# Expert matrices loaded with consecutive rows in one partition, in a two-block transformer kernel with a mixture of 64 experts

## The chip, the core and the metric

The kernel runs on one core of a Trainium2 chip, alone. The metric is device time in microseconds (us) of one execution. The core has a matrix engine (PE, with its own weight loads PEld), a vector engine (DVE), a scalar engine (ACT), GpSimd (POOL), a queue engine that issues most DMAs (SP), and 16 DMA engines that the queues share. SBUF has 128 partitions; a matmul contracts over partitions and writes one of eight PSUM banks.

## What is computed

A sequence of 256 tokens of width 1024 passes two blocks, all in float32. The first block and the mixer of the second are not touched. What matters is the last stage, a mixture of 64 experts with top-2 routing (`t` are the normalised tokens, `gate` the two routing weights):

```
hid = silu(t[tokens of e] @ w_gate[e]) * (t[tokens of e] @ w_up[e])      # 1024 -> 512
out[tokens of e] += gate * (hid @ w_down[e])                              # 512 -> 1024
```

`w_gate` and `w_up` are (64, 1024, 512), `w_down` is (64, 512, 1024): each matrix is 2 MB, 192 of them. A row of `w_gate` or `w_up` is 2 KB in DRAM, a row of `w_down` 4 KB, and a matrix is one contiguous block. A last normalisation follows.

## The kernel before

The first 40% of the time is dense work: 47 panels of weights go through `raw`, are split in two parts on ACT and DVE, and PE multiplies them (lines L763 and L1200). The change does not touch that.

The expert stage takes experts in **pairs**, 32 rounds. Every expert has 64 slots (`SLOTS`), so that a pair fills 128 rows; if an expert had more tokens a further pass would run, guarded by `fullest > SLOTS`. In this input none runs: each line of the loop shows 32 rounds. One round on PE, in `experts` from L1078 on, is, in program order:

- gate and up products (L1090): for each of two matrices, 8 chunks `k` of the width, 2 experts, 64 columns of `xeT` stationary and 512 columns of the matrix moving; the two experts use different halves of the PE columns. Before each matrix PE waits for its DMA (`pair_landed`).
- two transposes of `pick_g` (L1096), then, when DVE has multiplied the silu by the up product (`h_e`, L1652), **four transposes of `h_e`** (L1101): slice `c` is columns `128 c` to `128 c + 127` of the 512. ACT copies the result into `heT` (L708).
- `gather` for the next pair (L1072): 16 matmuls that pick the pair's tokens out of **`t_rows`** with a 0/1 matrix; chunk `k` of `xeT` is columns `128 k` to `128 k + 127` of `t_rows`.
- down products (L1112), four chunks `c` of `heT`, and, when both halves of `y_e` are copied out (L1659 on DVE, L712 on ACT), the scatter into the four accumulating banks (L1120).

`nc.tensor.transpose(out, in_, identity)` loads `in_` as the stationary operand (PEld LDWEIGHTS) and moves the identity.

Since chunk `k` of the stationary operand and chunk `k` of the matrix meet in one matmul, partition `p` of both must hold the same row of the matrix. Before, that row is `128 k + p`.

**Loads.** `load` on SP (L356 to L374) issues two DMAs, one for each expert of a pair, into `slots` (gate, up and down) or, for the gate matrices of odd rounds, into `areas`. Gate is so double-buffered and issued a round ahead of up and down, which have one buffer each. The order on SP is up, down, gate of the round after, each behind a wait that its buffer is free: up behind the last up product (L1090), down and gate behind the last down product (L1112). For all but the first two rounds the DMA has a condition: an expert without tokens is not loaded.

**`t_rows`** is made once (L1565): DVE multiplies the normalised rows `xn` by the gain, two instructions of 128x1024, after its part of the transposes for the router (L1188) and while PE runs the router's product (L1049). `t_ready` lets DVE go on to `choose`, and is one of two things for which the load of the second gate pair waits (the other is the router's product). Then come DVE's routing steps (L1570 to L1622), the first `choose` (L1634), the first gather, and the first round.

Of the kernel before, what the change touches and what calls it, by code (L numbers as in the profile page):

```python
# [22 lines left out]
ALU = mybir.AluOpType  # L23
# [3 lines left out]
P = 128  # L27
# [3 lines left out]
KT = D // P  # L31
# [57 lines left out]
def program(nc, x_in, p_in, norm_mix_g, w_in, w_sgu, b_sgu, ln_v_g, ln_v_b, rel_bias, w_out, norm_ffn_g,  # L89
# [24 lines left out]
    with ExitStack() as ctx:  # L114
# [29 lines left out]
        ident = sb("ident", [P, P])  # L144
# [28 lines left out]
        xn = rows_area(9)  # L173
# [28 lines left out]
        t_rows = rows_area(0)  # L202
        zeros = area(4)[:, 0:256].bitcast(mybir.dt.bfloat16)
        gains = rows_area(5)
        routerw = area(4)[:, 512:512 + KT * (EG + NE)].rearrange("p (k n) -> p k n", k=KT)
        xeT = area(1)[:, 0:1024].rearrange("p (k s) -> p k s", k=KT)
        h_e = area(1)[:, 1024:1536]
# [9 lines left out]
        banks = [ctx.enter_context(nc.psum_tensor(f"bank{b}", [P, 512], F32)) for b in range(8)]  # L217
# [87 lines left out]
        def expert_panel(w, e, odd):  # L305
            s = {"gate": 0, "up": 2, "down": 4}[w] + e
            place = area(6 + 2 * e, 2) if w == "gate" and odd else slots[:, s, :]
            return place.rearrange("p (k n) -> p k n", k=4 if w == "down" else 8)
# [12 lines left out]
        def _(sp):  # L321
# [15 lines left out]
            for q in range(2 * NP):  # L337
                p, (kind, j) = q // 2, PANELS[q // 2]
                k = shape(p)[0] // 2
# [19 lines left out]
            def load(w, i, pair, odd, beyond):  # L359
                weights, used = {"gate": (w_gate, gated), "up": (w_up, upped), "down": (w_down, downed)}[w]  # L360


                tokens = [None if beyond is None else tokens_of(pair, e) for e in range(2)]
                if isinstance(i, int) and i == 0:
                    sp.wait_ge(panel_done, NP)
                elif isinstance(i, int) and w == "gate":
                    sp.wait_ge(t_ready, 1)
                    sp.wait_ge(routed, 1)
                else:
                    sp.wait_ge(used, i - 1 if w == "gate" else i)  # L370
                for e in range(2):
                    cond = {} if beyond is None else {"cond": tokens[e] > beyond}
                    sp.dma_start(expert_panel(w, e, odd), weights[0, 2 * pair + e].rearrange("(k p) n -> p k n", p=P),
                                 **cond).then_inc(pair_landed["odd_gate" if w == "gate" and odd else w, e], 16)  # L374

            def tokens_of(pair, e):
# [353 lines left out]
        def _(pe):  # L730
            mm, turn_tile = nc.tensor.matmul, nc.tensor.transpose
# [108 lines left out]
            for g in range(GROUPS):  # L840
                last = turn_tile(banks[6 + g // 4][:, P * (g % 4):P * (g % 4) + P], w_s[:, g, :], ident[:, :])
# [8 lines left out]
            for m in range(MT):  # L850
                for half in range(2):
                    for g in range(4 * half, 4 * half + 4):
                        last = mm(banks[4 + 2 * m + half][:, P * (g % 4):P * (g % 4) + P], w_sT[:, g, :],
                                  v_rows[:, m, P * g:P * g + P], start=True, stop=True)
# [25 lines left out]
            for k in range(2):  # L880
                for m in range(MT):
                    last = turn_tile(banks[0][:, S * k + P * m:S * k + P * m + P], p_rows[:, m, P * k:P * k + P], ident[:, :])
            last.then_inc(p_turned, 1)
            for j in range(8):
                p = AT["ff2", j]
                pe.wait_ge(hid_ready, 4 * (j // 2) + 4)
                for k in range(KT):
                    if k % 4 == 0:
                        pe.wait_ge(w_ready, 2 * p + k // 4 + 1)
                    for m in range(MT):  # L890
                        last = product(banks[4 + 2 * m + j % 2][:, :], (hid_hi, hid_lo),
                                       (every, KT * (j // 2) + k, slice(P * m, P * m + P)), parts(p), (every, k, every),
                                       j < 2 and k == 0, j >= 6 and k == KT - 1)
# [3 lines left out]
            p = AT["pp", 0]  # L897
            pe.wait_ge(w_ready, 2 * p + 2)
            pe.wait_ge(pT_ready, 1)
            for half in range(2):  # L900
                for m in range(MT):
                    for k in range(2):
                        last = product(banks[4 + 2 * m + half][:, :], (pT_hi, pT_lo), (every, k, slice(P * m, P * m + P)),
                                       parts(p), (every, k, slice(512 * half, 512 * half + 512)), k == 0, k == 1)
# [9 lines left out]
            for k in range(KT):  # L914
                last = product(banks[4][0:HEADS, 0:S], (dtw_hi, dtw_lo), (every, k, every), h, (every, k, every),
                               k == 0, k == KT - 1)
# [3 lines left out]
            for m in range(MT):  # L920
                last = turn_tile(banks[4][:, S + HEADS * m:S + HEADS * m + HEADS], dt_cols[:, P * m:P * m + P],
                                 ident[0:HEADS, 0:HEADS])
# [3 lines left out]
            p = AT["kv2", 0]  # L926
            w, b0 = parts(p), pair_of(p)
# [6 lines left out]
            for m in range(MT):  # L934
                for k in range(KT):
                    last = product(banks[b0 + 1][:, P * m:P * m + P], h, (every, k, slice(P * m, P * m + P)),
                                   w, (every, k, slice(2 * P, 3 * P)), k == 0, k == KT - 1)
# [33 lines left out]
            for m in range(MT):  # L971
                for half in range(2):
                    for c in range(4):
                        last = turn_tile(banks[2 * m + half][:, P * c:P * c + P], xc[:, 4 * half + c, P * m:P * m + P],
                                         ident[:, :])
# [10 lines left out]
            for g in range(SSD_G):  # L986
                last = turn_tile(banks[0][:, P + P * g:P + P * g + P], xc[:, 8 + g, 0:P], ident[:, :])
            last.then_inc(sums_made, 1)

            for m in range(MT):  # L990
                for g in range(SSD_G):
                    last = mm(banks[1][:, 256 * m + P * g:256 * m + P * g + P], xc[:, 8 + g, P * m:P * m + P],
                              xc[:, 10 + g, P * m:P * m + P], start=True, stop=True)
# [20 lines left out]
            for m in range(MT):  # L1014
                for q in range(4):
                    n = 4 * m + q
                    if n >= 2:
                        pe.wait_ge(seg_ready, n - 1)
                    for i in range(4):
                        last = mm(banks[n % 2][:, P * i:P * i + P], a[:, m, 4 * q + i:4 * q + i + 1].to_broadcast([P, P]),  # L1020
                                  upper[:, :], start=True, stop=True)
# [7 lines left out]
            for g in range(SSD_G):  # L1029
                last = mm(banks[g][:, :], b_tok[:, g, :], xde[:, 512 * g:512 * g + 512], start=True, stop=True)  # L1030
# [3 lines left out]
            for g in range(SSD_G):  # L1034
                last = mm(banks[2 + g][:, :], xc[:, 10 + g, P:S], state[:, 512 * g:512 * g + 512], start=True, stop=True)
# [11 lines left out]
            for m in range(MT):  # L1047
                for k in range(KT):
                    last = mm(banks[0][:, 72 * m:72 * m + 72], hT[:, k, P * m:P * m + P], routerw[:, k, :],  # L1049
                              start=(k == 0), stop=(k == KT - 1))  # L1050
# [25 lines left out]
            def experts(half_i, odd, last_one=False):  # L1076

                i = 2 * half_i + odd  # L1078
                pe.wait_ge(xe_a, i + 1)
                pe.wait_ge(xe_d, i + 1)  # L1080

                for w, bank, done in (("gate", banks[2], gated), ("up", banks[3], upped)):
                    for e in range(2):
                        if w == "gate":
                            pe.wait_ge(pair_landed["odd_gate" if odd else w, e], 16 * (half_i + 1))
                        else:
                            pe.wait_ge(pair_landed[w, e], 16 * (i + 1))
                    for k in range(KT):
                        for e in range(2):
                            last = mm(bank[SLOTS * e:SLOTS * e + SLOTS, :], xeT[:, k, SLOTS * e:SLOTS * e + SLOTS],  # L1090
                                      expert_panel(w, e, odd)[:, k, :], start=(k == 0), stop=(k == KT - 1))
                    last.then_inc(done, 1)

                pe.wait_ge(picked_g, i + 1)
                for m in range(MT):
                    last = turn_tile(banks[1][:, P * m:P * m + P], pick_g[:, m, :, :].rearrange("p e s -> p (e s)"),  # L1096
                                     ident[:, :])
                last.then_inc(put_turned, 1)
                pe.wait_ge(he_ready, i + 1)
                for c in range(4):  # L1100
                    last = turn_tile(banks[0][:, P * c:P * c + P], h_e[:, P * c:P * c + P], ident[:, :])  # L1101
                last.then_inc(he_turned, 1)
                pe.wait_ge(heT_ready, i + 1)
                pe.wait_ge(put_ready, i + 1)
                if not last_one:
                    gather(i + 1)
                for e in range(2):
                    pe.wait_ge(pair_landed["down", e], 16 * (i + 1))
                for c in range(4):
                    for half in range(2):  # L1110
                        for e in range(2):
                            last = mm(banks[2 + half][SLOTS * e:SLOTS * e + SLOTS, :], heT[:, c, SLOTS * e:SLOTS * e + SLOTS],  # L1112
                                      expert_panel("down", e, odd)[:, c, 512 * half:512 * half + 512],
                                      start=(c == 0), stop=(c == 3))
                last.then_inc(downed, 1)
                pe.wait_ge(ye_a, i + 1)
                pe.wait_ge(ye_d, i + 1)
                for m in range(MT):
                    for half in range(2):
                        last = mm(banks[4 + 2 * m + half][:, :], put[:, m, :], y_e[:, 512 * half:512 * half + 512],  # L1120
                                  start=False, stop=False)
                last.then_inc(scattered, 1)
# [20 lines left out]
        def _(dve):  # L1143
# [418 lines left out]
            dve.wait_ge(xn_a, 5)  # L1562
            dve.wait_ge(gains_loaded, 32)
            for m in range(MT):
                last = tt(t_rows[:, m, :], xn[:, m, :], gains[:, 0, :], ALU.mult)  # L1565
            last.then_inc(t_ready, 1)

            dve.wait_ge(consts_made, 1)
# [155 lines left out]
```

## Time and profile before

| | |
|---|---|
| three runs, median (lowest to highest) | 1771.02 us (1770.88 to 1771.63) |
| the profiled execution, first to last instruction | 1770.0 us |
| what lies around that span, by the median | 1.0 us |
| PE busy, share of the span | 1610.4 us, 91% |
| DVE, ACT busy | 552.4 us, 455.6 us |
| expert stage, first product to last scatter | 752 to 1759 us |
| moved by DMA over the span | 489.17 MB |

The page gives no total of its own for the profiled execution besides its span; its own time is the span and what lies around it, and that is why the two stand side by side. In the rows further down, a time with x32 or x1024 is the time of a group; "idle before" names what ended the wait. A MATMUL of float32 operands appears as two records, a transpose as one. In the chain of waits each row starts where its predecessor released it.

### The profile page before, as it was taken

What the parts mean: (1) busy time and instruction counts of PE and PEld (TensorE: products, weight loads), DVE (VectorE), ACT (ScalarE), POOL (GpSimd) and SP (SyncE); (2) the same over time, 40 slices, a digit from 0 to 9 for tenths busy, and PEclk for the clock granted to TensorE, in tenths of its full rate; (3) what the DMA queues carried; (4) which work ended last, traced back from release to release, by engine and by line L of the source; (5) the groups of instructions that cost most, each with busy time, mean ns of one, the idle gap of its engine ahead of it and who ended that gap; (6) DMA issues with size and microseconds to landing.
All of it is one profiled execution on the core that took longest, in us unless ns stands there. A gap on an engine that the chain in (4) does not pass through costs nothing.

```text
span 1770.0 us, 21051 instructions
## 1 busy us (share of the span) xinstructions
PE 1610.4 (91%) x8473; PEld 987.1 (56%) x8475; DVE 552.4 (31%) x936; ACT 455.6 (26%) x652; POOL 13.5 (1%) x30
## 2 busy tenths in 40 slices
PE   7999889999799979699999999999999999999996
PEld 5897779987689767534343343433434334343342
DVE  5755565544647976401011010110101101001012
ACT  5435545432535553101111011110111101111011
POOL 1000000000000000000000000000000000000000
PEclk9999989999899979799999999999999999999999
DMA  7554235554332213789899999999999999998994
GB/s 277 186 198 141 96 119 185 191 191 166 131 131 96 96 53 97 290 323 337 321 392 393 397 392 396 394 392 397 392 395 395 392 397 329 379 368 287 395 392 156
DMA packets 213002, 489.17 MB, mean 276 GB/s; under 512 B 6424, under 2 KB 8596, under 8 KB 212949
## 3 DMA queue, kind: packets, MB, share of 16 engines
q1 hardware_dynamic: 211764, 484.17, 74.6%
q0 software_dynamic: 1184, 4.26, 0.8%
q8 instruction: 37, 0.61, 0.2%
q14 instruction: 17, 0.13, 0.0%
HBM read 506.20 MB, written 1.08 MB: 287 GB/s over the span
## 4 chain that ended last, share of the span: by engine, by line
PE 74%; DVE 9%; ACT 3%; issue 2%; DVEq 0%; ACTq 0%
PE bank L1090 25%; PE bank L763 18%; PE bank L1112 13%; PE bank L1072 7%; PE bank L1120 7%; DVE areas L1659 1%; DVE areas L1652 1%; PE bank L1101 1%; ACT areas L708 1%; DVE w_lo L1200 1%; DVE h_lo L1190 1%; PE bank L746 1%; DVE areas L1450 1%; PE bank L1020 1%; PE bank L1010 0%
## 5 line engine op out<-in xcount | busy, mean ns | idle before, releaser
L1090 PE MATMUL bank<-slots,areas 128*64 128x512 f32 x1536 | 335.8, 593 | 1.1 <-DVE areas L1644 1.1
L1090 PEld LDWEIGHTS bank<-slots,areas 128*64 128x64 f32 x1536 | 109.8, 137 | 221.9 <-issue 221.9
L1200 DVE TENSOR_TENSOR w_lo<-raw,w_hi 128x2048 fp32r<-128x2048 f32 (+2 forms) x98 | 209.0, 2167 | 75.9 <-ACT w_hi L508 75.7
L1112 PE MATMUL bank<-slots,areas 128*64 128x512 f32 x1024 | 226.8, 595 | 0.7 <-ACT areas L708 0.7
L1652 DVE TENSOR_TENSOR areas<-bank,areas 128x512 f32<-128x512 f32 x32 | 22.1, 692 | 556.5 <-PE bank L1090 556.5
L508 ACT ACTIVATE w_hi<-raw 128x2048 fp32r<-128x2048 f32 (+2 forms) x98 | 173.6, 1816 | 62.3 <-PE bank L763 56.5
L763 PE MATMUL bank<-h_hi,w_hi 128*128 128x256 f32 x560 | 160.9, 287 | 0.2 <-DVE h_lo L1190 0.2
L763 PE MATMUL bank<-h_lo,w_hi 128*128 128x256 f32 x560 | 159.1, 284 | 0.0
L763 PE MATMUL bank<-h_hi,w_lo 128*128 128x256 f32 x560 | 159.1, 284 | 0.0
L1072 PE MATMUL bank<-areas 128*128 128x128 f32 x1024 | 125.5, 282 | 26.3 <-ACT areas L708 23.7
L763 PE MATMUL bank<-w_hi,h_hi 128*128 128x512 f32 (+1 forms) x344 | 138.4, 402 | 7.9 <-DVE h_lo L1190 3.0
L1112 PEld LDWEIGHTS bank<-slots,areas 128*64 128x64 f32 x1024 | 70.7, 137 | 132.6 <-issue 127.9
L1120 PE MATMUL bank<-areas 128*128 128x512 f32 x256 | 117.5, 602 | 28.3 <-DVE areas L1659 28.3
L1072 PEld LDWEIGHTS bank<-areas 128*128 128x128 f32 x1024 | 119.5, 196 | 33.7 <-issue 30.0
L763 PE MATMUL bank<-w_hi,h_lo 128*128 128x512 f32 (+1 forms) x344 | 134.1, 390 | 0.0
L763 PE MATMUL bank<-w_lo,h_hi 128*128 128x512 f32 (+1 forms) x344 | 134.0, 390 | 0.0
L1090 PE MATMUL bank<-areas 128*64 128x512 f32 x512 | 113.4, 595 | 0.0
L763 PEld LDWEIGHTS bank<-h_hi,w_hi 128*128 128x128 f32 x560 | 108.2, 193 | 2.1 <-issue 0.6
L763 PEld LDWEIGHTS bank<-h_lo,w_hi 128*128 128x128 f32 x560 | 108.3, 193 | 0.0
L763 PEld LDWEIGHTS bank<-h_hi,w_lo 128*128 128x128 f32 x560 | 108.1, 193 | 0.0
L1120 PEld LDWEIGHTS bank<-areas 128*128 128x128 f32 x256 | 46.0, 189 | 101.5 <-ACT areas L712 55.6
L706 ACT ACTIVATE areas<-bank 128x512 f32<-128x512 f32 x32 | 19.1, 598 | 310.4 <-PE bank L1090 310.4
(293 smaller groups left out, 1452.0 us busy)
## 6 DMA issues: line engine op xcount, KB each, us to landing
slots<-in_w_up_dram SPq DMA_DIRECT2D x64, 2048.0 KB, 16.9
slots<-in_w_down_dram SPq DMA_DIRECT2D x64, 2048.0 KB, 14.2
slots<-in_w_gate_dram SPq DMA_DIRECT2D x32, 2048.0 KB, 19.2
areas<-in_w_gate_dram SPq DMA_DIRECT2D x32, 2048.0 KB, 22.0
raw<-in_w_in_dram SPq DMA_DIRECT2D x42, 1024.0 KB, 6.0
raw<-in_w_ff_dram SPq DMA_DIRECT2D x32, 1024.0 KB, 5.3
raw<-in_w_out_dram SPq DMA_DIRECT2D x12, 1024.0 KB, 5.2
raw<-in_w_ple_gate_dram SPq DMA_DIRECT2D x4, 1024.0 KB, 5.5
```

The source lines that it names most:

```text
L508: last = act_(hi, source, ACT.Copy)
L706: act_(h_e, banks[2][:, :], ACT.Silu).then_inc(silu_ready, 1)
L708: act_(heT.rearrange("p c s -> p (c s)"), banks[0][:, :], ACT.Copy).then_inc(heT_ready, 1)
L746: last = turn_tile(banks[b][:, at:at + P], src[:, m, P * k:P * k + P], ident[:, :])
L763: last = mm(psum, a[i][a_at], b[j][b_at], start=(start and n == 0), stop=(stop and n == 2))
L1020: last = mm(banks[n % 2][:, P * i:P * i + P], a[:, m, 4 * q + i:4 * q + i + 1].to_broadcast([P, P]), upper[:, :], start=True, stop=True)
L1072: last = mm(banks[b][:, P * k:P * k + P], t_rows[:, m, P * (4 * b + k):P * (4 * b + k) + P], pick[:, m, :, :].rearrange("p e s -> p (e s)" ...
L1090: last = mm(bank[SLOTS * e:SLOTS * e + SLOTS, :], xeT[:, k, SLOTS * e:SLOTS * e + SLOTS], expert_panel(w, e, odd)[:, k, :], start=(k == 0) ...
L1112: last = mm(banks[2 + half][SLOTS * e:SLOTS * e + SLOTS, :], heT[:, c, SLOTS * e:SLOTS * e + SLOTS], expert_panel("down", e, odd)[:, c, 51 ...
L1120: last = mm(banks[4 + 2 * m + half][:, :], put[:, m, :], y_e[:, 512 * half:512 * half + 512], start=False, stop=False)
L1200: last = tt(lo, source, hi, ALU.subtract)
L1652: tt(h_e, banks[3][:, :], h_e, ALU.mult).then_inc(he_ready, 1)
```

## The change

Three edits. Partition `p` of an expert matrix now holds rows `8 p` to `8 p + 7` (gate, up) or `4 p` to `4 p + 3` (down) instead of every 128th row. That is one run of 16 KB in DRAM and in SBUF instead of eight of 2 KB or four of 4 KB. To match, chunk `c` of `heT` holds the elements `4 p + c` of `h_e`, read by the transposes with a step of four float32 (16 bytes); and `t_rows` is stored permuted, so that its chunk `k` holds the elements `8 p + k`. The permutation is made by the multiplication at L1565, which reads both operands with a step of eight float32 (32 bytes) and writes in order. No instruction, wait or buffer is added or taken away.

```diff
@@ -370,7 +370,7 @@
                 for e in range(2):
                     cond = {} if beyond is None else {"cond": tokens[e] > beyond}
-                    sp.dma_start(expert_panel(w, e, odd), weights[0, 2 * pair + e].rearrange("(k p) n -> p k n", p=P),
+                    sp.dma_start(expert_panel(w, e, odd), weights[0, 2 * pair + e].rearrange("(p k) n -> p k n", p=P),
                                  **cond).then_inc(pair_landed["odd_gate" if w == "gate" and odd else w, e], 16)
@@ -1098,7 +1098,7 @@
                 for c in range(4):
-                    last = turn_tile(banks[0][:, P * c:P * c + P], h_e[:, P * c:P * c + P], ident[:, :])
+                    last = turn_tile(banks[0][:, P * c:P * c + P], h_e.rearrange("s (p c) -> s c p", c=4)[:, c, :], ident[:, :])
                 last.then_inc(he_turned, 1)
@@ -1562,7 +1562,8 @@
             for m in range(MT):
-                last = tt(t_rows[:, m, :], xn[:, m, :], gains[:, 0, :], ALU.mult)
+                last = tt(t_rows[:, m, :].rearrange("t (k p) -> t k p", k=KT), xn[:, m, :].rearrange("t (p k) -> t k p", k=KT),
+                          gains[:, 0, :].rearrange("t (p k) -> t k p", k=KT), ALU.mult)
             last.then_inc(t_ready, 1)
```

## Rows read from the trace of the kernel before

**Rows 1.** Waits of PE over the whole span: total us, times, longest us

```profile
PE bank L1120 <- DVE areas L1659: 28.3, 32, 0.9
PE bank L1072 <- ACT areas L708: 23.7, 31, 0.8
PE bank L1101 <- DVE areas L1652: 15.8, 32, 0.5
PE bank L831 <- DMA areas<-in_norm_ffn_dram: 10.6, 1, 10.6
```

**Rows 2.** Chain of waits, one round and the next start: start us, us, what

```profile
1225.72 13.91 PE bank L1090 x64
...
1239.72 0.70 DVE areas L1652
...
1240.47 0.67 PE bank L1101 x4
...
1241.16 0.61 ACT areas L708
...
1241.89 3.83 PE bank L1072 x32
1245.72 7.04 PE bank L1112 x32
...
1252.79 0.70 DVE areas L1659
...
1253.63 3.67 PE bank L1120 x8
1257.30 13.91 PE bank L1090 x64
```

**Rows 3.** DMA from 1029 to 1061 us: rate in 40 slices, packets, queue

```profile
GB/s 384 387 389 384 394 381 389 384 417 410 410 410 410 410 410 410 410 410 410 410 397 389 387 384 394 381 389 384 389 384 387 389 381 394 382 392 384 389 384 389
DMA packets 5230, 12.61 MB, mean 394 GB/s; under 512 B 96, under 2 KB 96, under 8 KB 5230
...
q1 hardware_dynamic: 5230, 12.61, 104.3%
```

**Rows 4.** Engines, clock and DMA by stretch, 911.6 to 1445 us

```profile
911.60:1445.00 533.40, 496.89 (x2405) 210.04 (x2402) 52.21 (x102) 62.42 (x85) 0.00 (x0) 1.00 1.04 394
```

**Rows 5.** SP's up and gate issues, start us, us; landings by window

```profile
892.58 1.82 SPq L373 DMA_DIRECT2D slots<-in_w_up_dram  x2
slots<-in_w_up_dram SPq DMA_DIRECT2D x2, 2048.0 KB, 15.6
...
1414.83 11.31 SPq L373 DMA_DIRECT2D slots<-in_w_gate_dram  x2
...
1432.24 5.04 SPq L373 DMA_DIRECT2D slots<-in_w_up_dram  x1
slots<-in_w_up_dram SPq DMA_DIRECT2D x1, 2048.0 KB, 19.3
...
1447.05 0.91 SPq L373 DMA_DIRECT2D areas<-in_w_gate_dram  x2
```

**Rows 6.** Chain of waits, the round whose up matrices those are

```profile
1446.77 13.91 PE bank L1090 x64
```

**Rows 7.** Timeline, DVE and PE around the making of `t_rows`

```profile
726.86 2.35 DVE L1565 TENSOR_TENSOR areas<-areas 128x1024 f32<-128x1024 f32 x2
...
727.63 3.76 PE L1049 MATMUL bank<-areas,hT 128*128 128x72 f32 x32 [0.98 <-DVE hT L1188]
...
731.50 0.31 DVE L1570 COPY areas<-bank 128x144 f32<-128x144 f32 x1 [2.29 <-PE bank L1049]
...
737.68 12.54 SPq L373 DMA_DIRECT2D areas<-in_w_gate_dram  x2
```

**Rows 8.** DVE by shape: two reduces of 128 elements, in order and strided

```profile
L1255 DVE TENSOR_REDUCE peak<-soft 128x1 f32<-128x128 f32 x32 | 8.8, 276 | 0.0
...
L1592 DVE TENSOR_REDUCE areas<-areas 128x16 f32<-128x128 f32 x1 | 0.4, 380 | 0.0
```

**Rows 9.** Weight loads by shape in one round, 1190 to 1230 us: busy us, mean ns

```profile
L1072 PEld LDWEIGHTS bank<-areas 128*128 128x128 f32 x32 | 3.6, 192 | 1.0 <-issue 1.0
...
L1101 PEld LDWEIGHTS bank<-ident,areas 128*128 128x128 f32 x4 | 0.4, 141 | 0.7 <-DVE areas L1652 0.7
```

**Rows 10.** Source line L1101: duration ns min/median/max of its matmuls

```profile
L1101 PE MATMUL bank<-ident,areas x128: 272/273/331, 766.8 to 1746.0; 128*128 128x128 f32 x128
```

**Rows 11.** The page's DMA queues: packets, MB, share of 16 engines

```profile
q1 hardware_dynamic: 211764, 484.17, 74.6%
```

## The prediction

> **What bounds the kernel now.** I read the waits of PE first, because PE is busy for 91% of the span. In the expert stage its three largest waits are for engines that have just been handed its own result, 0.5 to 0.9 us each, 32 times [rows 1]. The only DMA in the list is a small vector at the start of the kernel (L831). PE does not wait for an expert matrix once.
>
> The chain of waits says the same for one round [rows 2]: from 1225.72 to 1257.30 us, 31.58 us, it is products on PE for 29.1 us (13.91 + 0.67 + 3.83 + 7.04 + 3.67), three copies or multiplications of 0.6 to 0.7 us on DVE and ACT, and small gaps. No DMA stands in it, and 32 such rounds are some 57% of the span.
>
> Next I asked how close the DMA is behind. In one saturated round the queues move at 381 to 397 GB/s (mostly 387) while gate and up pass, whose runs are 2 KB, and at 410 while down passes, with runs of 4 KB [rows 3]. The mean is 394 GB/s, also over seventeen rounds at once, with the engines' share at 104% (packets overlap a little) [rows 3, 4]. A round needs six matrices of 2.097 MB, 12.58 MB; at 394 that is 31.94 us. PE asks for them every 31.58 us. **The DMA is 1% too slow, and this cannot be seen in PE's waits because it is bought from a reserve.** The last up transfer of this stretch is issued at 1432.24 and lands 19.3 us later [rows 5], at 1451.5; its product begins in the middle of the block that starts at 1446.77 [rows 6], at 1446.77 + 6.96 = 1453.7. So 2.2 us of reserve are left. Seventeen rounds earlier the pair issued from 892.58 on lands 15.6 us after issue [rows 5], the second about 1 us behind the first, so at some 909; its product begins at 1453.7 - 17 x 31.58 = 916.8: a reserve of 8 us. It falls by 5.8 / 17 = 0.34 us a round, which is 31.94 - 31.58 again. Then, at 1447, two gate issues take 0.91 us instead of 11.31 [rows 5]: I read this as a load left out for an expert without tokens, after which the queue catches up. The reserve runs low, and never out.
>
> **The DMAs.** 192 transfers change their runs from 2 or 4 KB to 16 KB. Per engine a run of 2 KB takes 2048 x 16 / 387 = 84.7 ns, one of 4 KB takes 4096 x 16 / 410 = 159.8 ns. The second 2 KB cost 75.1 ns, which leaves 9.6 ns for each run. My estimate from these two: 16 KB take 9.6 + 8 x 75.1 = 610 ns, 430 GB/s, and a round's matrices take 29.3 us instead of 31.9. The lower bound of the gain is nothing: the queue may cut the runs as before. In the span either is worth **0 us**, because no product waits now. What covers the transfers is PE's 31.58 us; if the cover were gone they would cost the 0.34 us by which a round's 31.94 exceed it. SP issues as many DMAs in the same order behind the same waits. It would be held less long by a full queue (1 to 12 us per pair now), which nobody waits for.
>
> **`t_rows`.** The two DVE instructions end at 726.86 + 2.35 = 729.21. The next DVE instruction starts at 731.50, when PE's router product lets it [rows 7]. So 2.29 us are free. The step of 32 bytes has one relative in the trace: the reduce at L1592 reads 128 elements with that step and takes 380 ns, one of 128 elements in order (L1255) takes 276 [rows 8]. That is 104 / 128 = 0.81 ns per element (some of it may be its 16 outputs instead of one). For 2 x 1024 elements it makes 1.66 us if the two strided operands are read side by side: hidden. If they add up it is 3.32 us, of which 1.03 come onto the path, once. I take 0; bounds 0 and 1.0. The load behind `t_ready` waits for the same router product and is issued at 737.68 because the queue is full, so it does not move.
>
> **The transposes of `h_e`.** The four are on the chain, 0.67 us in each round [rows 2]. What changes is their weight load, now with a step of 16 bytes; the identity moves as before. A load takes 141 ns by its record, and those of the gather, of the same 128 columns but for a float32 product, 192 [rows 9]. The first of the four matmuls takes 0.33 us by its record (the maximum) [rows 10], so the others follow at (0.67 - 0.33) / 3 = 0.11 us, and the gather's at (3.83 - 0.33) / 31 = 0.11 as well [rows 2]: the longer load of the gather costs no pace. So a load 51 ns longer costs next to nothing per matmul, since it runs ahead under the one before; only the first of four, which waits for DVE, shows it. If a strided load takes as long as the gather's: 51 ns and 3 ns allowed for each of the other three make 0.06 us a round, 32 rounds, **2.0 us**. Lower bound: 0, no penalty. Upper bound: DVE's 1.81 ns per strided element, as if the memory set it. That is 1.00 in order, (1175 - 276) / (1024 - 128) from half of the 2.35 us and the 276 ns [rows 7, 8], plus 0.81. Then a load takes 128 x 1.81 = 232 ns, 122 more than the pitch of 110 for three of them; the first shows 232 less 53 (128 columns at one clock of 2.4 GHz, the granted clock being 1.00 [rows 4]), 179. That is 0.55 us a round, 18 us. I take 2.0, because the gather's loads are the nearest row: the same engine, the same port, at a lower pace per column.
>
> Row first, then the rule: no row of PE has a step, so the trace is silent on it. The Trainium skill (SBUF — State Buffer, under Door 1: The DMA port swizzle) says that SBUF has lines of 16 bytes, that two hits on a line are needed to hide the access, and that a new line for each access pays a penalty. By that rule all the `h_e` loads and the `t_rows` reads pay; the size is not given. The same paragraph also calls a stride of four float32 free, and by that only `t_rows` pays. DVE's 380 against 276 ns agrees with a penalty at 32 bytes.
>
> **Sum.** 0 + 0 + 2.0 = 2.0 us on the profiled execution: span 1770.0 to 1772.0, and with the 1.0 us around it 1773.0. The median shown, 1771.02, is that execution's span plus the same 1.0, so it serves as the base.
>
> **Rivals.**
> - *The strided loads leave their cover (slower).* Place: L1101, each round. Point: when a load takes more than about 0.11 us of the PE's port, because then three of four matmuls wait too. At DVE's extra 0.81 ns on top of one clock, 0.42 ns, a column, a load takes 157 ns: 104 + 3 x 47 = 0.25 us a round, 8 us, **1779 us**. At the upper bound **1789**. For: DVE shows a penalty, and PE would read faster than DVE. Against: loads run ahead, and a moderate penalty is covered. (It is what the Trainium skill's rule of lines, named above, would do here if its penalty is large.)
> - *The long runs are slower (slower).* Neighbouring partitions are then read 16 KB apart instead of 2 or 4, and their streams may meet in DRAM. The reserve of 8 us lasts 17 rounds as long as a round's matrices take under 31.58 + 8 / 17 = 32.05 us; it decides below 12.58 / 32.05, 392 GB/s. At 385 they take 32.7 us: 17 x 1.1 - 8, **+11 us**, 1782. Against: down, with longer runs, is the faster one now.
> - *The change does not reach the engines.* Runs are cut into 2 KB packets again and strides cost nothing: **1771.0**. Inside the forecast.
> - *Faster.* A shorter DMA stretch pays only if a product waits. Even if all of the 2.2 us reserve had been a hidden wait, it would be **1769**. Nothing in the waits speaks for it.
>
> **How the numbers follow.** A measurement of this kernel can tell about 0.2%, 3.5 us, from no change. Forecast (0 to 3.5 us slower, the third rival in it): 0.67. Loads out of their cover: 0.22. Long runs slower: 0.06. Faster by over 3.5 us: 0.05, for what I have overlooked. Slower is 0.22 + 0.06 = 0.28. The range 1770 to 1783 holds the forecast and the rivals up to half of their ends; some 0.16 lie outside. The forecast's own range is 1770 to 1774.5.
>
> **What would show it.** Right: packets on the queue fall from 211764 [rows 11] to under 100000, the DMA share in a round falls below 1.0, SP's issues get short, the block of 13.91 us stays as it is, L1101's matmuls take 0.67 to 0.75 us, L1565 takes 2.4 to 4.6 and DVE's wait before L1570 shrinks by as much. Wrong: L1101 over 0.8 us a round; a DMA among PE's waits; rounds under 31.5 us; or a matmul of L1090 that is quicker beside less traffic.

## The result, and the profile after

The changed kernel takes 1774.18 us (median of 20 runs, 1772.44 to 1776.99); the kernel before took 1771.22 in its 20 (1769.23 to 1774.10). The ratio is **1.0019, 95% interval 1.0012 to 1.0025**: 3 us slower. That is within the 0.2% that the prediction counts as no change, but twenty runs of each tell it from none. The forecast was 1773.0.

The chain of waits of the changed kernel, one round and the next start (start us, us, what), shows where it is:

```profile
1224.93 13.91 PE bank L1090 x64
...
1238.93 0.70 DVE areas L1653
...
1239.68 0.76 PE bank L1101 x4
...
1240.46 0.61 ACT areas L708
...
1241.19 3.83 PE bank L1072 x32
1245.03 7.04 PE bank L1112 x32
...
1252.09 0.70 DVE areas L1660
...
1252.93 3.67 PE bank L1120 x8
1256.60 13.91 PE bank L1090 x64
```

A round takes 31.67 us instead of 31.58, and one row differs from [rows 2]: L1101, 0.76 for 0.67. 32 x 0.09 = 2.9 us, which is the difference of the medians. (The spans of the two profiled executions, 1770.0 and 1770.8, differ by less because the dense stage of the second happened to end 2.2 us earlier: L1570 started at 731.50 before [rows 7], the same copy at 729.34 after.)

Weight loads and matmuls of L1101 by source line (duration ns min/median/max) answer to [rows 9, 10]:

```profile
L1101 PEld LDWEIGHTS bank<-ident,areas x128: 196/211/220, 764.6 to 1746.7; 128*128 128x128 f32 x128
L1101 PE MATMUL bank<-ident,areas x128: 283/284/387, 764.6 to 1746.8; 128*128 128x128 f32 x128
```

A load takes 70 ns more. The first matmul shows most of it (387 against 331), the others 11 ns each. DVE around `t_rows`, by timeline, answers to [rows 7]:

```profile
724.74 3.95 DVE L1565 TENSOR_TENSOR areas<-areas 128x1024 f32<-128x1024 f32 x2
729.34 0.31 DVE L1571 COPY areas<-bank 128x144 f32<-128x144 f32 x1 [0.65 <-PE bank L1049]
```

The two instructions take 1.60 us more together, and all of it comes out of the wait behind them, 2.29 us before and 0.65 now.

The DMA did what the change says. The page's queue row, and the stretches 1033.5 to 1048 us (no pause in it) and 911.6 to 1445 us (last three numbers: granted clock, DMA share, GB/s), to set beside [rows 11, 3, 4]:

```profile
q1 hardware_dynamic: 79028, 484.17, 68.8%
...
1033.50:1048.00 14.50, 14.50 (x66) 4.84 (x66) 0.00 (x0) 0.60 (x1) 0.00 (x0) 1.00 1.01 432
...
911.60:1445.00 533.40, 496.86 (x2397) 211.85 (x2394) 52.21 (x102) 62.42 (x85) 0.00 (x0) 1.00 0.95 397
```

The page has 211764 - 79028 = 132736 packets less. An expert's three matrices were 2560 runs and are now 384, 2176 less, and 132736 is 61 x 2176: each run of 16 KB is one packet, and 61 of the 64 experts are loaded, which bears out the prediction's reading that some loads are left out. A pair of gate issues on SP takes 1.01 us (at 1191.80), where the kernel before was held 9.83 (at 1192.75).

432 GB/s while it runs (I had 430), so a round's 12.58 MB need 29.1 us and the engines now pause, 95% instead of 104%. The mean stays at 397 because PE asks for no more. PE's busy time in the long stretch is 496.86 us for 496.89 before. The Trainium skill (DMA: Bandwidth & Descriptors, Specifications) gives 435 GB/s as the ceiling of the SBUF side: the 432 agree. It also gives some 358 GB/s as the limit of the memory side per core; with one core at work both kernels are over that.

### The profile page after: what moved, and what is told of

It reads as the page before. It is cut to its first block, busy times and chain, and to the rows that moved or that the text cites. A ratio compares the mean times of both kernels' runs of the same rounds, so it can differ in the third digit from the quotient of the medians.

```text
span 1770.8 us, 21053 instructions
## 1 busy us (share of the span) xinstructions
PE 1610.3 (91%) x8475; PEld 988.9 (56%) x8475; DVE 554.2 (31%) x936; ACT 455.5 (26%) x652; POOL 13.5 (1%) x30
## 3 DMA queue, kind: packets, MB, share of 16 engines
q1 hardware_dynamic: 79028, 484.17, 68.8%
## 4 chain that ended last, share of the span: by engine, by line
PE 74%; DVE 9%; ACT 3%; issue 2%; DVEq 0%; ACTq 0%
PE bank L1090 25%; PE bank L763 18%; PE bank L1112 13%; PE bank L1072 7%; PE bank L1120 7%; PE bank L1101 1%; DVE areas L1653 1%; DVE areas L1660 1%; ACT areas L708 1%; DVE w_lo L1200 1%; DVE h_lo L1190 1%; PE bank L746 1%; DVE areas L1450 1%; PE bank L1020 1%; PE bank L1010 0%
## 5 line engine op out<-in xcount | busy, mean ns | idle before, releaser
L1072 PE MATMUL bank<-areas 128*128 128x128 f32 x1024 | 125.5, 282 | 26.3 <-ACT areas L708 23.7
L1072 PEld LDWEIGHTS bank<-areas 128*128 128x128 f32 x1024 | 119.5, 195 | 32.2 <-issue 28.6
```

Source lines behind the costliest of these rows:

```text
L1072: last = mm(banks[b][:, P * k:P * k + P], t_rows[:, m, P * (4 * b + k):P * (4 * b + k) + P], pick[:, m, :, :].rearrange("p e s -> p (e s)" ...
```

## The experiments

**Which part costs, and does the rest do anything?** `loads_only` takes the new loads and puts the two reads back in order; `reads_only` is the other half. In both the operands don't match row for row, so the expert part of the output is another; the work is the same.

```diff
 loads_only, against the changed kernel
-                    last = turn_tile(banks[0][:, P * c:P * c + P], h_e.rearrange("s (p c) -> s c p", c=4)[:, c, :], ident[:, :])
+                    last = turn_tile(banks[0][:, P * c:P * c + P], h_e[:, P * c:P * c + P], ident[:, :])
...
+                last = tt(t_rows[:, m, :], xn[:, m, :], gains[:, 0, :], ALU.mult)
 reads_only, against the changed kernel
-                    sp.dma_start(expert_panel(w, e, odd), weights[0, 2 * pair + e].rearrange("(p k) n -> p k n", p=P),
+                    sp.dma_start(expert_panel(w, e, odd), weights[0, 2 * pair + e].rearrange("(k p) n -> p k n", p=P),
```

> All matrices are loaded in runs of 16 KB, but the transposes of h_e and the making of t_rows read in order as before, so the operands no longer match row for row: the result is another, the work is the same. Theory Reads (the strided weight loads at L1101 are the whole difference, 0.09 us in each of 32 rounds, and the DMA is worth nothing because no product waits for it): rounds of 31.58 us, L1101 0.67 us, time as before, 1771 within noise. Rival Loads (the long runs themselves slow the stage, for instance by writing 16 KB at a time into a partition that PE reads): rounds of 31.67 us with L1101 at 0.67, time some 3 us over before. Both: DMA at about 432 GB/s while busy, share in a round about 0.95.

> The loads are those of the kernel before (runs of 2 and 4 KB), the transposes and t_rows read with their steps: operands don't match row for row, the work is the same. Theory Reads: rounds of 31.67 us, L1101 0.76 us, weight loads 211 ns, time 3 us (0.17%) over before. The DMA still runs at 394 GB/s, but loses only 31.94 - 31.67 = 0.27 us of reserve a round instead of 0.34. Rival Loads: rounds of 31.58, time as before.

Measured: `loads_only` 1771.36 us, ratio 1.0003 (0.9994 to 1.0012); `reads_only` 1774.42, ratio 1.0015 (1.0006 to 1.0024), each against 1771.46 for the kernel before beside them. The intervals overlap slightly; the chains decide. `loads_only`, one round:

```profile
1224.25 13.91 PE bank L1090 x64
...
1239.00 0.67 PE bank L1101 x4
...
1255.84 13.91 PE bank L1090 x64
```

and `reads_only`:

```profile
1226.95 13.91 PE bank L1090 x64
...
1241.70 0.77 PE bank L1101 x4
...
1258.62 13.91 PE bank L1090 x64
```

Rounds of 31.59 and 31.67. The long runs neither help nor disturb; the reads are the difference.

**Which of the two reads?** `down_old` leaves `w_down` in its old layout, so that `h_e` is transposed in order, and keeps the permuted `t_rows`. Its result is unchanged.

```diff
 down_old, against the changed kernel
+                    sp.dma_start(expert_panel(w, e, odd), weights[0, 2 * pair + e].rearrange("(k p) n -> p k n" if w == "down" else "(p k) n -> p k n", p=P),
...
+                    last = turn_tile(banks[0][:, P * c:P * c + P], h_e[:, P * c:P * c + P], ident[:, :])
```

> Gate and up in runs of 16 KB with t_rows permuted once, down as before in runs of 4 KB, and so h_e is transposed in order. Theory Reads: the whole penalty goes (rounds 31.58, L1101 0.67), the time is that of before, 1771, while the DMA keeps most of its relief: four matrices at 432 and two at 410 GB/s make 29.7 us of a round, against 29.1 with all six. Rival t_rows (its 0.8 us longer instructions cost something further on): over before by up to 1.6 us, with the routing steps starting later.

Measured: 1771.14 us, ratio 1.0002 (0.9993 to 1.0011). One round of its chain:

```profile
1223.34 13.91 PE bank L1090 x64
...
1238.09 0.67 PE bank L1101 x4
...
1254.92 13.91 PE bank L1090 x64
```

Rounds of 31.58 and L1101 at 0.67, as before. `t_rows` takes 2024 ns an instruction and costs nothing. So the 3 us are the strided weight loads of L1101 alone.

**What is it about the step?** `step2` lays `w_down` out in runs of 8 KB and reads `h_e` with a step of 8 bytes, with an unchanged result; `step3` reads elements `3 p + c` of `h_e`, 12 bytes apart, which are not the right ones.

```diff
 step2, against the changed kernel
+                    sp.dma_start(expert_panel(w, e, odd).rearrange("p (h r) n -> p h r n", r=2 if w == "down" else 8),
+                                 weights[0, 2 * pair + e].rearrange("(h p r) n -> p h r n", p=P, r=2 if w == "down" else 8),
...
+                    last = turn_tile(banks[0][:, P * c:P * c + P], h_e.rearrange("s (h p r) -> s h r p", h=2, r=2)[:, c // 2, c % 2, :], ident[:, :])
 step3, against the changed kernel
+                    last = turn_tile(banks[0][:, P * c:P * c + P], h_e[:, 0:384].rearrange("s (p c) -> s c p", c=3)[:, min(c, 2), :], ident[:, :])
```

> Down in runs of 8 KB: partition p holds rows 2p and 2p+1 of each half of the matrix, so the transposes of h_e read with a step of two float32, 8 bytes. If two hits on a line of 16 bytes are enough (so the Trainium skill, SBUF — State Buffer): weight loads stay at 141 ns, rounds 31.58, time as before. If any step costs: weight loads up to 211 ns, rounds up to 31.67, time up to 3 us over before. DMA share as in the changed kernel.

> As the changed kernel, but the transposes of h_e read elements 3p, 3p+1 and 3p+2 (the fourth repeats the third), a step of 12 bytes: other numbers, same work. If the cost is a new line for an access, three of four reads meet one: weight loads between 141 and 211 ns, about 190. If the penalty is a switch at a step of 16 bytes: 141. If it is a switch at any step above one: 211.

Measured: `step2` 1774.53 us, ratio 1.0014 (1.0005 to 1.0023); `step3` 1773.44 in its one run, which lies inside the range of the kernel before beside it (1769.35 to 1773.81) and settles nothing about the time; its load records do bear on the question. Weight loads by shape from 1190 to 1230 us (busy us, mean ns), first `step2`, where the line is L1102:

```profile
L1102 PEld LDWEIGHTS bank<-ident,areas 128*128 128x128 f32 x4 | 0.6, 208 | 0.7 <-DVE areas L1654 0.7
```

then `step3`:

```profile
L1101 PEld LDWEIGHTS bank<-ident,areas 128*128 128x128 f32 x4 | 0.6, 205 | 0.7 <-DVE areas L1653 0.7
```

Steps of 4, 8, 12 and 16 bytes: 141, 208, 205 and 211 ns. Over these steps it looks like a switch between "in order" and "not", and not a matter of how many reads fall in one line of memory. Longer steps were not run on this engine. The rule of two hits on a line, which the prediction cites from the Trainium skill (SBUF — State Buffer), would leave 8 bytes free: for these weight loads the measurement says otherwise, and at 16 bytes it speaks against the same page's count of four float32 as free.

**Can another engine permute for less?** `dve_write` lets the multiplication that makes `h_e` write it permuted into `y_e`, which is free then. Its result is unchanged.

```diff
 dve_write, against the changed kernel
-                tt(h_e, banks[3][:, :], h_e, ALU.mult).then_inc(he_ready, 1)
+                tt(y_e[:, 0:512].rearrange("s (c p) -> s p c", c=4), banks[3][:, :].rearrange("s (p c) -> s p c", c=4),
+                   h_e.rearrange("s (p c) -> s p c", c=4), ALU.mult).then_inc(he_ready, 1)
...
+                    last = turn_tile(banks[0][:, P * c:P * c + P], y_e[:, P * c:P * c + P], ident[:, :])
```

> As the changed kernel, but the permutation of h_e is made by the multiplication on DVE (L1653), which reads in order and writes with a step of 512 bytes between neighbours into y_e (free at that time), and the transposes read in order. L1101 goes back to 0.67 us. If DVE's writes pay 0.8 ns per element as its reads do, L1653 goes from 0.69 to 1.1 us, rounds to 32.0, time 10 to 13 us over before. If strided writes are free: rounds of 31.58, time as before, and the transposes' 3 us are won back.

Measured: 1797.97 us (1791.70 to 1804.37), ratio 1.0160 (1.0136 to 1.0183), twice the expected loss. Its chain of waits, in two rounds:

```profile
1245.67 1.04 DVE areas L1653
...
1246.75 0.67 PE bank L1101 x4
...
1248.18 3.83 PE bank L1072 x32
...
1275.76 1.74 PE bank L1090 x8
...
1277.59 1.04 DVE areas L1653
...
1278.67 0.67 PE bank L1101 x4
...
1280.10 5.46 PE bank L1072 x32
```

The write pays: 1.04 us for 0.70, 0.34 more in each round, 11 us. L1101 is back at 0.67. The second part was in no expectation: in some rounds the gather takes 5.46 us for 3.83. The engines' busy times of that stretch say why (the third number from the right is the granted clock):

```profile
1280.00:1286.00 6.00, 5.90 (x36) 5.50 (x38) 0.41 (x1) 0.60 (x1) 0.00 (x0) 0.72 1.01 429
```

The granted clock is 0.72 of 2.4 GHz on average there, because PE ran part of it at its lower level of 1.2 GHz. The same view of two microseconds in the middle of the gather shows that level alone:

```profile
1281.00:1283.00 2.00, 2.00 (x12) 2.00 (x11) 0.00 (x0) 0.00 (x0) 0.00 (x0) 0.50 1.04 442
```

In the chains of the other kernels the gather takes 3.83 or some 3.58 us in every full round. Before this gather PE had only 0.44 us of transposes of `pick_g` and 0.67 us of transposes of `h_e` between 1277.50, where the up products end, and 1280.10. The profiled execution has seven such gathers: 7 x 1.63 = 11 us, and 11 + 11 makes its span, 1789.9, out of 1767.4 for `down_old`. The other 24 gathers follow the same waits and the same transposes and keep the clock at 1.00, so what decides between the two is not shown. The spread of this kernel's runs goes with the clock: the mean granted clock was 0.970, 0.968, 0.966 and 0.963 in the executions of 1791.70, 1797.19, 1798.75 and 1804.37 us. Only the first of them has a trace that shows where.

**What is the headroom worth?** `short_old` and `short_new` are the kernel before and the changed one without the second half of the scatter (tokens 128 to 255 get no expert part).

```diff
-                for m in range(MT):
+                for m in range(1):
                     for half in range(2):
                         last = mm(banks[4 + 2 * m + half][:, :], put[:, m, :], y_e[:, 512 * half:512 * half + 512],
```

> The kernel before, with only the first half of the scatter: the matmuls for tokens 128 to 255 at L1120 are left out in every round, so a round of PE is 4 x 0.43 us, 1.7 to 1.8, shorter, 29.8 us. Its output lacks the experts' part for those tokens. Theory: the reserve of some 8 us is then used up by 31.94 - 29.8 = 2.1 us a round, in about four rounds, and from there on PE waits for a matrix in most rounds until loads are left out: rounds near 31.9, some 18 x 2.1 - 8 = 30 us lost; time 1771 - 57 + 30 = 1744. If the DMA is further from the limit than I reckon: 1714.

> The changed kernel with the same half of the scatter left out. A round of PE is 29.9 us, and its six matrices take 12.58 MB / 432 GB/s = 29.1: no wait for a matrix, time 1774 - 57 = 1717, some 27 us under the same cut in the kernel before. If the DMA's rate falls when it is busy all the time (the mean is 397 now, with pauses): waits appear and the two are closer than 10 us.

Measured: `short_old` 1751.43 us (ratio 0.9886, 0.9870 to 0.9903), `short_new` 1719.24 (0.9703, 0.9687 to 0.9719). The same cut brings 55 us in the new layout and 20 in the old. Waits of PE from 760 us on (total us, times, longest), `short_old`:

```profile
PE bank L1090 <- DMA slots<-in_w_up_dram: 28.8, 16, 1.9
...
PE bank L1112 <- DMA slots<-in_w_down_dram: 1.6, 1, 1.6
```

`short_new` has no DMA among its waits. Two starts in its chain:

```profile
1230.82 13.91 PE bank L1090 x64
...
1260.78 13.91 PE bank L1090 x64
```

Its rounds take 29.96 us, 1.71 under 31.67. Without its waits `short_old` should stand at 1771.4 - 32 x 1.71 = 1716.7; it lost 35 us, of which the rows show 30.4. Another 2.2 us lies in the products: the 32 behind such a wait take 7.10 us in the chain, where half of the undisturbed 13.91 is 6.96, and 16 x 0.14 = 2.2. Some 2 us stay unplaced.

**A version that uses it.** The chain shows a wait that a change of order fills: PE waits 0.77 us for ACT's copy of `heT` (L1072 in [rows 1]: 23.7 us in all) although only the gather's first half needs the bank that it frees. In the three `reorder` kernels PE gathers bank 1 first and waits for `heT` only ahead of bank 0. `reorder_mix` is this on `down_old`, `reorder_new` on the changed kernel, `reorder_old` on the kernel before. Their results are unchanged.

```diff
+                for b in (1, 0):
+                    if b == 0 and not first:
+                        pe.wait_ge(heT_ready, i)
                     for k in range(4):
...
-                pe.wait_ge(heT_ready, i + 1)
                 pe.wait_ge(put_ready, i + 1)
                 if not last_one:
                     gather(i + 1)
...
-                act.wait_ge(gathered, 2 * i + 1)
+                act.wait_ge(gathered, 2 * i + 2)
...
-                dve.wait_ge(gathered, 2 * i + 2)
+                dve.wait_ge(gathered, 2 * i + 1)
```

> down_old (gate and up in runs of 16 KB, down in runs of 4 KB, h_e transposed in order) with one wait taken off PE's path: the gather's second half (into bank 1, free once put is copied) is put ahead of the wait for heT, its first half (bank 0) behind it. PE's 0.77 us wait of each round ahead of L1072 is then filled, rounds 31.58 - 0.77 = 30.8 us; the matrices need 29.7, so nothing waits for a DMA: 31 x 0.77 = 24 us less, 1747. If the wait only moves to another place (the copies of the gather on ACT and DVE, or the down matrices), it stays near 1771.

> The same order of PE in the changed kernel as it stands: 31.67 - 0.77 = 30.9 us a round, no wait for a DMA, 1774 - 24 = 1750, 3 us over the version with down in its old layout.

> The same order of PE in the kernel before, all loads in runs of 2 and 4 KB. A round of PE is 30.8 us, the matrices need 31.94: 1.1 us of reserve lost a round, the 8 us gone in seven, and from there on PE waits for matrices, some 18 x 1.1 - 8 = 12 us in all by my reckoning, more if I go by short_old, where 37 us were lost instead of the 30 reckoned: 1759 to 1763. The new layout is then worth 10 to 15 us where it was worth nothing before. If it comes out at 1747 as well, the reserve is larger than I think.

Measured, against 1771.43 for the kernel before beside them: `reorder_mix` **1740.87 us**, ratio 0.9830 (0.9816 to 0.9844); `reorder_new` 1742.19, 0.9835 (0.9821 to 0.9849); `reorder_old` 1755.29, 0.9910 (0.9896 to 0.9924). One round of `reorder_mix` in its chain of waits:

```profile
1222.72 0.70 DVE areas L1656
...
1223.46 0.66 PE bank L1103 x4
1224.12 3.58 PE bank L1074 x32
1227.71 7.04 PE bank L1115 x32
...
1253.28 0.70 DVE areas L1656
```

30.56 us, 1.02 less: the copy of `heT` is off the chain, gaps included (0.75), and the gather follows the transposes without a start of its own (3.58 for 3.83), which I had not counted. 31 x 1.02 = 31.6; 30.6 measured. In `reorder_old` PE waits for the up matrices again:

```profile
PE bank L1092 <- DMA slots<-in_w_up_dram: 13.8, 12, 1.2
```

which is nearly all of the 14.4 us between it and `reorder_mix`. So here the new layout of gate and up is worth 0.8%, and it was worth nothing to the kernel as it stood. All three came out 4 to 8 us under what was expected, mostly for the gather's shorter start.

Between `reorder_mix` and `reorder_new` the medians differ by 1.3 us where 3 were expected; the intervals overlap, and five runs don't settle that. The traces do show the cost of the strided loads. In the chain of `reorder_new`:

```profile
1228.22 0.75 PE bank L1103 x4
...
1258.87 0.74 PE bank L1103 x4
```

That is 0.75 for 0.66 us, and a round of 30.65 for 30.56. From the first to the last product of L1092 it is 963.4 us against 960.9, so 2.5 us in the expert stage.

## Why the prediction was right

**What bounds the kernel.** PE, with no wait for an expert matrix, and a reserve that a DMA 1% too slow was eating. `loads_only` shows the first (nothing gained from 432 GB/s), the two `short` kernels and `reorder_old` the second: with PE's rounds some 29.9 and 30.6 us long matrices in the old layout come late, while at 31.58 the reserve lasted. The reckoning of the reserve (8 us, then the difference of the two periods in each round) gave 30 us lost for `short_old`, where 35 were lost, and 12 for `reorder_old`, where it was 14.

**The DMAs.** 0 us in the sum, and 0 measured. The rate worked out from the two run lengths was 430 GB/s, and 432 was measured.

**`t_rows`.** 0 in the sum. Extra time per element 0.78 ns, (2017 - 1218) / 1024, where L1592 gave 0.81; the two strided operands are read side by side. With 1.60 of 2.29 us used the cover held. `down_old`, with this reading in it and the time of the kernel before, shows that it costs nothing.

**The transposes.** This term was mis-sized, though only by 1 us: 2.0 predicted, 2.9 measured. A load became 70 ns longer (the gather's row had made it 51), the first of four showed 56 of them, and the others took 11 ns each where 3 were allowed. 56 + 3 x 11 = 89 ns, 32 times. So a load 70 ns longer is nearly hidden behind the matmul before it, as the gather's rows had suggested, but not wholly.

**The rivals.** The first rival's price was too high: by DVE's 0.81 ns per element each load would be 104 ns longer, and it is 70, or 0.55 per element. But its mechanism is not refuted. By its own reckoning a load would need the port for one clock a column and the penalty, 53 + 70 = 123 ns, 13 over the pitch of 110, and the second to fourth matmul each come 11 ns later than before, at (0.76 - 0.387) / 3 = 0.124 us instead of 0.113; the gather's loads, at 53 + 51 = 104, are under the pitch and cost none. So these loads seem to stand just at the edge of their cover. No run varies the penalty (the steps of 8, 12 and 16 bytes give 205 to 211 ns), so this is an argument and not shown. That the penalty was small enough for the forecast of 2.0 us is luck in part: no row of PE had a step, and 51 ns was borrowed from loads that differ in another way. The long runs are faster, not slower. The change reached the engines. Nothing became faster, for the reason given there.

**The signs.** Packets, DMA share, SP's issues, L1565, the wait behind it and the block of 13.91 us came out as named. L1101 took 0.76 us, just over the 0.67 to 0.75 that was to mean right, and under the 0.8 that was to mean wrong.

**The base.** The 1.0 us "around the span" is the median of three runs less the span of one execution. Wherever the time and the span of the same execution are both known they differ by 1.7 to 1.9 us. The base of 1771.02 is a measured median, and the forecast does not depend on the 1.0.

## What to carry to other kernels

Before paying for a faster transfer, compare its period with that of the engine that uses it, not its wait: here 31.94 against 31.58 us, no wait in sight, gain zero; and after one wait was taken off PE the longer runs of gate and up were worth 14 us. Put the permutation that a new layout needs where it is done once under cover (`t_rows`) and avoid it where it stands in every round on the chain (`h_e`): with gate and up in the new layout and down in the old one the DMA still has a pause in each round (its share is 0.97) and PE pays nothing.

## What the runs showed of the hardware that I had not expected

- A weight load of 128 float32 columns for a transpose takes 141 ns in order and 205 to 211 ns with a step of 8, 12 or 16 bytes.
- DVE's multiplication of 128x512 with a permuted write takes 1.03 us for 0.69, 0.66 ns per element, about what strided reads cost.
- The kernel with a DVE instruction 0.34 us longer lost 0.83 us a round in the median (26.5 us over 32 rounds). In its profiled execution the granted clock was at its lower level at the start of 7 gathers, each time behind the transposes and the waits for DVE and ACT, and each cost 1.63 us. Behind the same waits it stayed up in the other 24. In the kernel before, with the wait 0.34 us shorter, it stays at 1.00 [rows 4].
- 16 KB runs move at 432 GB/s where 2 KB runs moved at 387 and 4 KB runs at 410, and PE's matmuls (13.91 us for 64) are the same beside either.
